# Twelve projection tiles and the feed forward projections of the last block computed across: weights held, tokens moving

## The reference, cut to what matters

```python
def second_block(x, c, ...):
    sh1, sc1, ga1, sh2, sc2, ga2 = ...            # six rows of 1024 from c @ w_ada + b_ada
    xn = rms_norm(h, g_mix) * (1.0 + sc1) + sh1
    proj = jnp.dot(xn, w_in) + b_in               # 1024 x 5448
    q, k, v, qi, ki, wi, xr, yr, gate_a, gate_b = jnp.split(proj, cuts, axis=-1)
    attn = dsa_attention(q, k, v, qi, ki, wi, rel_bias)   # top 64 of the index scores
    xr = causal_dwconv(xr, conv_rnn_w, conv_rnn_b)        # 4 taps along the tokens
    rnn = rg_lru(xr, w_rg, b_rg, w_ig, b_ig, lam) * jax.nn.gelu(yr)
    merged = sigmoid(gate_a) * (attn @ w_o_attn) + sigmoid(gate_b) * (rnn @ w_o_rnn)
    h = h + ga1 * jnp.dot(merged, w_out)
    xn = rms_norm(h, g_ffn) * (1.0 + sc2) + sh2
    up = causal_dwconv(jnp.dot(xn, w_up), conv_ffn_w, conv_ffn_b)   # 1024 x 5632, 3 taps
    val, gte = jnp.split(up, 2, axis=-1)
    return rms_norm(h + ga2 * jnp.dot(silu(gte) * val, w_down), g_final)
```

## Time and profile before

| | us |
|---|---|
| median of three runs | 1084.53 |
| the profiled execution: its own time / its span | 1086.36 / 1084.3 |
| TensorE busy (5180 matmuls) | 1026.4 |
| VectorE busy | 732.6 |
| ScalarE busy | 585.8 |
| GpSimd busy | 115.6 |
| TensorE's share of the chain that ended last | 73% |

### The profile page before, as it was taken

The page is one execution under the profiler, slowest core; times in us unless marked ns, Lnnn a source line. Parts: engine busy times, 40 slices in busy tenths (PEclk is TensorE's granted clock), DMA queues, the critical chain, the costliest instruction groups (busy, mean ns, idle before and its releaser), DMA issues.

```text
span 1084.3 us, 13459 instructions
## 1 busy us (share of the span) xinstructions
PE 1026.4 (95%) x5180; PEld 850.1 (78%) x5180; DVE 732.6 (68%) x986; ACT 585.8 (54%) x842; POOL 115.6 (11%) x168
## 2 busy tenths in 40 slices
PE   6897999999999989899999999997999999999996
PEld 4675878889888777788888878886877788888885
DVE  5567775566346577578888666769766765777753
ACT  6657554444335567544443354577656456676641
POOL 0112140000000022200000011013630000000001
PEclk9999999999999999999999989999999999999998
DMA  9765479555556432389999796535465535554431
GB/s 348 274 170 73 136 202 303 188 181 174 194 175 197 157 113 76 101 287 352 353 325 320 295 317 215 166 121 165 147 213 206 163 112 184 191 193 156 175 136 39
DMA packets 98190, 213.98 MB, mean 197 GB/s; under 512 B 5440, under 2 KB 12880, under 8 KB 94736
## 3 DMA queue, kind: packets, MB, share of 16 engines
q1 hardware_dynamic: 93424, 196.39, 53.2%
q0 software_dynamic: 4416, 16.51, 6.3%
q10 hardware_dynamic: 288, 0.23, 0.1%
HBM read 208.39 MB, written 6.15 MB: 198 GB/s over the span
## 4 chain that ended last, share of the span: by engine, by line
PE 73%; DVE 11%; ACT 8%; issue 4%; DMA 2%; POOL 1%; SPq 0%; DVEq 0%; ACTq 0%; POOLq 0%
PE bank L883 22%; PE bank L885 22%; PE bank L884 22%; ACT hi L1199 4%; DVE lo L1634 4%; PE bank L861 3%; PE bank L898 1%; PE bank L863 1%; ACT junk L1062 1%; DMA raw<-in_w_in_a 1%; DVE early L1465 1%; DVE xres L1508 1%; DMA raw<-in_w_gate_up 1%; DMA early<-in_memT 1%; PE bank L944 0%
## 5 line engine op out<-in xcount | busy, mean ns | idle before, releaser
L1634 DVE TENSOR_TENSOR lo<-raw,hi 128x2048 fp32r<-128x2048 f32 (+1 forms) x164 | 366.9, 2240 | 215.7 <-ACT hi L1199 215.1
L1199 ACT ACTIVATE hi<-raw 128x2048 fp32r<-128x2048 f32 (+1 forms) x164 | 303.7, 1855 | 184.2 <-PE bank L885 144.0
L883 PE MATMUL bank<-hi,xTh 128*128 128x512 f32 (+2 forms) x896 | 346.8, 387 | 2.6 <-DVE lo L1634 2.2
L885 PE MATMUL bank<-hi,xTl 128*128 128x512 f32 (+2 forms) x896 | 337.7, 377 | 0.0
L884 PE MATMUL bank<-lo,xTh 128*128 128x512 f32 (+2 forms) x896 | 337.7, 377 | 0.0
L883 PEld LDWEIGHTS bank<-hi,xTh 128*128 128x128 f32 x896 | 170.6, 190 | 33.7 <-DVE lo L1634 2.8
L885 PEld LDWEIGHTS bank<-hi,xTl 128*128 128x128 f32 x896 | 170.2, 190 | 31.7
L884 PEld LDWEIGHTS bank<-lo,xTh 128*128 128x128 f32 x896 | 170.5, 190 | 28.5
L883 PE MATMUL bank<-hi,hTh 128*128 128x512 f32 x264 | 103.5, 392 | 0.2 <-DVE lo L1634 0.2
L885 PE MATMUL bank<-hi,hTl 128*128 128x512 f32 x264 | 102.8, 389 | 0.0
L884 PE MATMUL bank<-lo,hTh 128*128 128x512 f32 x264 | 102.8, 389 | 0.0
(11 more groups left out here) (346 smaller groups left out, 1315.2 us busy)
## 6 DMA issues: line engine op xcount, KB each, us to landing
raw<-in_w_gate_up SPq DMA_DIRECT2D x44, 1024.0 KB, 6.4
raw<-in_w_down SPq DMA_DIRECT2D x30, 1024.0 KB, 5.1
raw<-in_w_ada SPq DMA_DIRECT2D x24, 1024.0 KB, 6.2
raw<-in_w_up SPq DMA_DIRECT2D x22, 1024.0 KB, 5.1
raw<-in_w_in SPq DMA_DIRECT2D x21, 1024.0 KB, 5.0
raw<-in_w_out SPq DMA_DIRECT2D x12, 1024.0 KB, 5.1
raw<-in_w_in_b SPq DMA_DIRECT2D x10, 1024.0 KB, 5.1
raw<-in_w_in_a SPq DMA_DIRECT2D x6, 1024.0 KB, 11.9
```

Source lines behind the costliest of these rows:

```text
L883: e.matmul(o, sh, h[:, k, :], start=p.first and k == 0, stop=False)
L885: done = e.matmul(o, sl, h[:, k, :], start=False, stop=p.last and k == p.nk - 1)
L1199: e.activation(hi_s[m % SPLITS][:, 0:n], raw[p.at % RAWS][:, 0:n], ACT.Copy).then_inc(hi_made, 1)
L1634: e.tensor_tensor(lo_s[s][:, 0:n], raw[p.at % RAWS][:, 0:n], hi_s[s][:, 0:n].bitcast(F), ALU.subtract).then_inc(lo_made, 1)
```

## The change

Twelve tiles of 256 columns (`ACROSS`: the two halves of qi, q, both xr and both yr) and all of `w_up`, now in 22 tiles of 256, are computed *across*: the matmul holds 128 columns of the weights and moves the 256 tokens, so that the sum comes out with features on partitions, in the very bank that the step behind it reads. A tile is then one part with two chunks of 24 matmuls (one per 128 features), has one bank, and needs neither staging nor turning. The biases of q, qi and xr are added by ScalarE in place in the bank, two instructions and a wait for them (`with_bias`); they arrive as 16 more columns of `vectors`. kw, kv and the gates stay as they were.

```diff
-UP2 = tiles_of(DFF)[-1:] + tiles_of(DFF)[:-1]
+UP2 = [(c, 256) for c in [2560] + list(range(0, 2560, 256))]
+ACROSS = {768: ("qi", 0), 1024: ("qi", 2), 1352: ("conv", 0, 0), 1608: ("conv", 0, 2), 2376: ("gelu", 0, 0), 2632: ("gelu", 0, 2),
+          1864: ("conv", 1, 0), 2120: ("conv", 1, 2), 2888: ("gelu", 1, 0), 3144: ("gelu", 1, 2), 0: ("q", 0), 256: ("q", 2)}
...
     for _, c, w, _ in IN2:
-        plan += [("in2", x) for x in columns(a["w_in_2"][0], c, w)]
+        for c_, w_ in [(c, 256), (c + 256, 256)] if c in ACROSS else [(c, w)]:
+            plan += [("in2", x) for x in columns(a["w_in_2"][0], c_, w_)]
...
+        if t.bank:
+            self.take(t.bank)
+            self.summed_by[t.bank] = t
+            return t
...
+            def across(p, ch, h, lo, xh, xl):
+                if ch == 0:
+                    await_bank(e, p.tile.bank)
+                o, at = x_bank(p.tile.bank)[:, ch * 256:ch * 256 + 256], slice(ch * 128, ch * 128 + 128)
+                for k in range(8):
...
+                    e.matmul(o, h[:, k, at], xh[:, k, :], start=k == 0, stop=False)
+                    e.matmul(o, lo[:, k, at], xh[:, k, :], start=False, stop=False)
+                    done = e.matmul(o, h[:, k, at], xl[:, k, :], start=False, stop=k == 7)
+                done.then_inc(part_done if ch else acc_first, 1)
...
-                elif kind in ("qi", "q"):
-                    e.wait_ge(acc_dve, order.tile_of["in2", kind, 768 if kind == "qi" else 0].d1)
-                    turned(claim(step), blocks_of(staged2_slot(kind), name[0] * 128, 2))
...
-                elif kind == "conv":
-                    c = (1352, 1864)[name[0]]
-                    e.wait_ge(acc_dve, in2_tile[c].d1)
-                    turned(claim(step), blocks_of(staged2_slot(c), name[1] * 128, 2))
-                elif kind == "gelu":
-                    c = (2376, 2888)[name[0]]
-                    e.wait_ge(acc_act, in2_tile[c].a1)
-                    e.wait_ge(acc_dve, in2_tile[c].d1)
-                    turned(claim(step), blocks_of(staged2_slot(c), name[1] * 128, 2))
...
-                elif kind == "cvT":
-                    _, c, what, k = name[0]
-                    e.wait_ge(acc_act, order.tile_of["raw", what, c].a1)
...
-                    turned(claim(name[0]), blocks_of(slot, k * 128, 2))
...
-                    for t in range(2):
-                        e.wait_ge(*full[t])
-                        e.activation(nrm_halves[n % 2][:, t, 0:w], pair[t][:, 0:w], ACT.Copy).then_inc(acc_act, 1)
...
+            def with_bias(name, columns):
+                e.wait_ge(*summed(name))
+                for j in range(2):
+                    x = x_bank(name)[:, j * 256:(j + 1) * 256]
+                    e.activation(x, x, ACT.Identity, bias=columns[:, j:j + 1]).then_inc(on_act, 1)
+                    n = own.up()
+                e.wait_ge(on_act, n)
...
                 elif kind in ("qi", "q"):
                     k = name[0]
+                    with_bias(step, bias_q[kind][:, k:k + 2])
                     high_of(step, qy[2][0][:, k:k + 2, :], two(x_bank(step)), 0.125)
...
                 elif kind == "conv":
                     half, k = name
-                    e.wait_ge(x_full, filled(step))
+                    with_bias(step, bias_xr[:, 4 * half + k:4 * half + k + 2])
```

More of the change, by code:

```diff
@@ L120, in __init__ @@
         self.chunks = (2 * nk + 3) // 4
+        if tile.bank:
+            self.chunks = 2
 class AccTile:
@@ L129, in __init__ @@
         self.m = None
+        self.bank = ACROSS[c] if kind == "across" else ("cv", c, l, 0) if kind == "raw" else None
 class Order:
@@ L238, in put @@
         elif kind == "conv":
-            self.turn(task, ON_D)
-        elif kind in ("gelu", "rgate"):
+            self.empty(task, ON_D)
+        elif kind == "gelu":
+            self.empty(task, ON_A)
+        elif kind == "rgate":
             self.turn(task, ON_A)
@@ L361, in part @@
         for ch in range(p.chunks):
-            for n in range(4 * ch, min(4 * ch + 4, 2 * nk)):
-                self.need((source, k0 + n % nk))
+            for k in range(8) if tile.bank else [k0 + n % nk for n in range(4 * ch, min(4 * ch + 4, 2 * nk))]:
+                self.need((source, k))
             self.steps.append(("mm", m, ch))
@@ L371, in part @@
             tile.m = m
+            if tile.bank:
+                self.turn_at[tile.bank] = (None, None, None)
     def evacuate(self, t):
@@ L379, in evacuate @@
                 self.need(task)
+        if t.bank:
+            if t.kind == "raw":
+                self.later.append(t.bank)
+            return
         self.steps.append(("evac", t.j))
@@ L511, in run @@
         for what, c, w, between in IN2:
-            self.linear("yr" if what == "yr" else "in2", what, c, w, 1 if w <= 256 else 2, ("z", 0), 0, between)
+            if c not in ACROSS:
+                self.linear("in2", what, c, w, 1 if w <= 256 else 2, ("z", 0), 0, between)
+                continue
+            self.linear("across", what, c, 256, 1, ("z", 0), 0, between[0:1])
+            for name in between[1].split():
+                self.named(name)
+            self.linear("across", what, c + 256, 256, 1, ("z", 0), 0, between[2:3])
         for c in (0, 512):
@@ L652, in build @@
         rate = small[:, 136:144]
+        wi = small[:, 96:112].rearrange("p (t h) -> p t h", t=2)
         m8 = small[:, 16:32]
@@ L730, in filled, with summed @@
             return order.turn_at[name][0] + 1
+        def summed(name):
+            return part_done, order.summed_by[name].m + 1
         def emptied(name):
@@ L1530, in evacuate @@
                     project(t_, pair, full)
-                elif kind == "yr":
-                    before = staged2[staged2.index(c) - 2]
-                    e.wait_ge(x_full, filled(end_of[before]))
-                    if before == "kw":
-                        e.wait_ge(wi_made, 1)
-                    e.wait_ge(*full[1])
-                    e.tensor_copy(staged2_slot(c)[:, 1, 0:w], pair[1][:, 0:w]).then_inc(acc_dve, 1)
                 elif kind == "orn":
```

75 lines of the change are left out of this document (30 added, 45 removed).

## The result

The change makes the kernel slower: 1089.73 us (median of 5, 1088.97 to 1092.37) against 1084.53 (median of 5, 1083.51 to 1086.95). The ratio is 1.0049, with a 95% interval of 1.0027 to 1.0070. A second measurement gave 1.0048 (1.0032 to 1.0063). That is +5.2 us where -3.6 was forecast, and outside the range.

A forecast was written before the change was run, and what follows sets the result against it. TensorE was taken as the sole bound in `w_up`, but in `w_in` only together with ScalarE and VectorE. Terms -4.3, -0.9 and +1.6 gave -3.6 us from 1084.53: 1080.9, called 1081.0, range 1077.5 to 1085.5.

The forecast's parts named there:

- The 16 more columns of `vectors`: At the start: the wider `vectors` was counted as 5% of one small load, costing nothing.
- `w_up` and `w_down`: -4.3: Ten periods of narrow parts, 11.52 us in place of 11.85, save 3.3 us; the first tile's two turns save 1.0.
- no wait on `lo`: In `w_up`: TensorE was expected to show no waits on `lo`; such waits would mean ScalarE was the bound there.
- The rival of the weight loads: Narrow matmuls: loads come out from behind them, gain gone at 0.1223 us a matmul, 1090 at 0.126; chance 0.05.
- the turns that were partly free: Removed turns: with half of each 0.485 us hidden, 34 turns bring 8 us less, 1089; chance 0.03.
- ScalarE's and VectorE's way to kv: -0.9: In `w_in`: kv's copies end some 0.9 us earlier than 755.9; bounds -2.5 and +1.
- The pairs of additions: 1.0 to 1.1 us each: ScalarE in `w_in`: the length expected for each pair of bias additions.
- the first rival: The wait at kv eats more: pairs cost 1.3 us, kv's turn behind 756, `w_in` +2.3, 1082.5; chance 0.25.
- The clock behind kv's turn: +1.6: Behind kv's turn in `w_in`: 3.3 us at half pace on TensorE lose 1.6 us; bounds 0 and 2.
- The sum: Whole kernel: -4.3 - 0.9 + 1.6 = -3.6 us against the median of 1084.53.
- forecast +0.7: The forecast net cost of the across tiles in `w_in`, from -0.9 on the way to kv and +1.6 for the clock.

The follow-up runs named there:

- a_pad: The changed kernel with 13 small statistics tensors packed into one, 64 bytes less, so tensors behind regain their old places; 0.9986 of the kernel before, 1084.37 us.
- up_only: The kernel before with `w_up` alone computed across, `vectors` and all places unchanged; 0.9963 of the kernel before.
- a_pad_x1: a_pad with GpSimd's scaling of the residual made to wait until VectorE has split the last piece of z; 0.9960 and again 0.9963 of the kernel before.
- in_x1: The changed kernel with `w_up` as before, places restored, and GpSimd's residual scaling waiting for the last split of z; 1.0015 of the kernel before.
- a_sweep: a_pad with hT alone displaced: layer 0 by 32 bytes, layer 1 by 192, the last block by 64; one execution took 1094.24 us.
- a_sweep2: a_pad with hT alone displaced: layer 0 by 96 bytes, layer 1 by 160, the last block by 224; one execution took 1089.55 us.
- b_m64: The kernel before with the statistics tensors packed into 192 columns, moving every tensor behind down by 64 bytes; 1.0017 of the kernel before.
- b_m128: The kernel before with the statistics tensors packed into 176 columns, moving every tensor behind down by 128 bytes; 1.0029 of the kernel before.

## Why the prediction was wrong

- **"The 16 more columns of `vectors` at the start are 5% of one small load: nothing."** This is the step that failed. I costed the columns as a load and not as 64 bytes in the allocation ahead of hT, qy and rTl. It measured +6.8 us (the change against `a_pad`), more than the whole forecast gain, and at least 4.3 of it lies in the three stages that hold hT, whose products the change doesn't touch.
- **What moves on a queue that was only relieved.** I counted the additions that VectorE loses and not the bias rows that GpSimd loses with them. Its scaling of the residual starts 2.7 us behind z's first turn, where it was 18.8, beside the split of z: +1.6 to +2.8 us, from the fix in three comparisons. The prediction has no term for the split of z at all.
- **`w_up` and `w_down`: -4.3.** Right: -4.0 in `up_only`; in the traces -3.3 to `w_down` (132.26 to 128.96) and -0.9 in it (60.58 to 59.64). The pace of 0.120 held, no wait on `lo` came behind the one at the second part (0.94 us, and 0.95 there before), and the form of the loads cost nothing. The rival of the weight loads is out. So is the one of the turns that were partly free.
- **ScalarE's and VectorE's way to kv: -0.9.** It measured +1.4 in the first profile. Step by step, behind z's first turn: ScalarE's `hi` (L1211, 721.50) came 0.2 us earlier, not 1.4, as it now waited for TensorE to be through with its part; the root was at 89.11 and 88.96 before, where I had 0.9 less, since the pair of additions (0.77) took what the copy gave; then the product took 1.9 more. I had written that GpSimd's product "now overlaps all of" the `lo`, and took the gain without asking which of the two would wait. The repetition of the same kernel had the `hi` 1.9 us earlier than before and the turn at 111.47, so up to 1.7 us of such a number differ from one execution to the next. What both executions share is the way behind that `hi`: 38.8 us to the turn, 37.2 before. That is +1.6 where my steps have +0.5 (1.4 earlier, then 0.9), and the product's 1.9 more than covers the 1.1 between the two.
- **The pairs of additions: 1.0 to 1.1 us each.** They took 0.77 to 0.81. By its sign (kv's turn behind 756, it stood at 760.26) the first rival came, but not by its cause, pairs of 1.3 us.
- **The clock behind kv's turn: +1.6.** It was low as forecast (0.50 from 761 to 763), but the premise that TensorE "is the bound again until the attention" was wrong: the wait for `acc` 33 us later gives most of it back. From the turn to the end of that wait it is 33.56 us after and 33.13 before, 0.4 in place of 1.6.
- **The sum.** Without the two missed costs (`a_pad_x1`: 0.9960 and 0.9963, -4.2 us) it comes near the forecast's -3.6. Of this `w_up` is all; `w_in` across gave between nothing and a loss (`in_x1` +1.6, interval -0.3 to +3.5; forecast +0.7).

Open is how much of the fix of GpSimd's scaling each execution keeps, and why a displacement of 192 bytes costs a third of what its neighbours do. A version that beats both kernels is `a_pad_x1`, the whole change with the places restored and that one wait; `up_only` is as fast, within the intervals, with far fewer edits.

## What to carry to other kernels

A tensor made a little wider moves every tensor allocated behind it: compare the pace of products in stages that the change doesn't touch, and restore the places before judging the change. When an instruction is taken off an engine, ask what is next on each queue that waited for it, and beside whom that will now run. Time lost on the main engine, as to a lower clock, costs only what its next wait for another chain doesn't give back.

## What the runs showed of the hardware

- The place of a held tensor in SBUF changes the pace of 512 column products from 0.227 us to as much as 0.234: 5.5 to 7 ns a product at six of seven displacements in steps of 32 bytes (modulo 256), 2 ns at the seventh (192; `a_sweep`, `a_sweep2`, `b_m64`, `b_m128`). It follows the held tensor alone (`a_sweep`).
- Of a VectorE subtraction with both inputs in SBUF and a GpSimd product, the one that started second ended as if it had waited for the first to end, at a lead of 0.96 us (before, the product first) as at one of 0.22 (after, the `lo` first): the order decided who lost 1 to 2 us. Four short subtractions, 1.42 us together, took 3.61 beside two scalings of some 1.1 us each.
- VectorE's additions out of PSUM (L1584) and GpSimd's product ran side by side at full length before (741.22 for 1.26, 741.44 for 2.35).
- The granted clock behind one and the same wait was 1.00 in one execution and 0.50 for 5 us in another (`a_pad_x1` and `a_pad`), and it fell to 0.50 in kw with no wait in the 8 us ahead of it (`a_pad_x1`).
